# Hybrid encoder trunk, float32 in split halves: a wait ahead of the fourth weight tile's load, and two memory tiles rounded on VectorE

## The reference

```python
mem_n = rms_norm(mem, mem_norm)                     # 256 x 2048
for layer in range(DEPTH):                          # DEPTH = 2
    mem_k, mem_v = jnp.split(mem_n @ w_mem_kv[layer], 2, axis=-1)   # each 256 x 512
    ...  # layer 0: RMSNorm, input projection, conv + gated linear recurrence,
         #          memory attention, output projection, residual, shared K/V
    ...  # layer 1: the same frame with stick-breaking attention on the shared K/V
return rms_norm(h, final_norm)
```

## Time and profile before

| what | us |
|---|---|
| median of 3 runs | 1472.4 |
| lowest and highest of them | 1471.49, 1472.69 |
| the profiled execution | 1472.62 |
| its span, first to last instruction | 1470.5 |
| PE busy in the span | 1460.9 (99%) |
| DVE busy | 998.5 (68%) |
| ACT busy | 716.3 (49%) |

### The profile page before, as it was taken

The page is one execution under the profiler, slowest core; times in us unless marked ns, Lnnn a source line. Parts: engine busy times, 40 slices in busy tenths (PEclk is TensorE's granted clock), DMA queues, the critical chain, the costliest instruction groups (busy, mean ns, idle before and its releaser), DMA issues.

```text
span 1470.5 us, 18202 instructions
## 1 busy us (share of the span) xinstructions
PE 1460.9 (99%) x6840; PEld 1220.9 (83%) x6840; DVE 998.5 (68%) x1317; ACT 716.3 (49%) x1065; POOL 122.7 (8%) x184
## 2 busy tenths in 40 slices
PE   9999999999999999999999999999999999999997
PEld 7888888888888888888888888888888888888886
DVE  6775568465576896856578676566566556578987
ACT  6764544444544545763325654433333423455465
POOL 0001111111110000000010001111111111100000
PEclk9999999999999999999999999999999999999999
DMA  9877778776796887477999876777887977879853
GB/s 341 292 285 221 162 209 237 172 241 149 195 257 176 324 319 264 153 262 277 362 343 356 286 223 218 239 214 177 237 238 197 255 188 216 246 223 328 315 200 143
DMA packets 154190, 357.97 MB, mean 243 GB/s; under 512 B 7825, under 2 KB 23441, under 8 KB 150033
## 3 DMA queue, kind: packets, MB, share of 16 engines
q1 hardware_dynamic: 103824, 205.98, 40.3%
q0 software_dynamic: 29376, 102.77, 28.5%
q10 hardware_dynamic: 20928, 48.41, 9.0%
HBM read 310.99 MB, written 113.25 MB: 289 GB/s over the span
## 4 chain that ended last, share of the span: by engine, by line
PE 99%; DMA 1%; SPq 0%; ACT 0%; DVE 0%; issue 0%
PE main L2115 24%; PE main L2114 24%; PE main L2113 24%; PE aux L2114 5%; PE aux L2115 5%; PE aux L2113 5%; PE aux L2475 2%; PE aux L2421 2%; PE aux L2417 2%; PE aux L2419 2%; PE main L2421 1%; PE main L2417 1%; PE main L2419 1%; PE aux L2464 1%; DMA w_raw<-in_w_mem_kv 1%; PE aux L2257 0%
## 5 line engine op out<-in xcount | busy, mean ns | idle before, releaser
L2113 PE MATMUL main<-act_hi,w_hi 128*128 128x512 f32 x1216 | 475.5, 391 | 0.0
L2115 PE MATMUL main<-act_hi,w_lo 128*128 128x512 f32 x1216 | 473.9, 390 | 0.0
L2114 PE MATMUL main<-act_lo,w_hi 128*128 128x512 f32 x1216 | 473.6, 389 | 0.0
L2115 PEld LDWEIGHTS main<-act_hi,w_lo 128*128 128x128 f32 x1216 | 228.2, 188 | 47.9
L2114 PEld LDWEIGHTS main<-act_lo,w_hi 128*128 128x128 f32 x1216 | 228.4, 188 | 46.8
L2113 PEld LDWEIGHTS main<-act_hi,w_hi 128*128 128x128 f32 x1216 | 228.4, 188 | 46.6
L1320 DVE SCALAR_TENSOR_TENSOR w_lo<-w_raw,gains,w_hi 128x512 fp32r<-128x512 f32 x180 | 123.3, 747 | 120.9 <-ACT w_hi L698 120.9
L698 ACT ACTIVATE w_hi<-w_raw,gains 128x512 fp32r<-128x512 f32 x180 | 115.4, 712 | 141.1 <-PE main L2115 125.7
L1311 DVE TENSOR_TENSOR w_lo<-w_raw,w_hi 128x1024 fp32r<-128x1024 f32 x88 | 104.2, 1223 | 94.0 <-ACT w_hi L691 93.8
L691 ACT ACTIVATE w_hi<-w_raw 128x1024 fp32r<-128x1024 f32 x88 | 88.5, 1057 | 153.1 <-PE main L2115 109.5
L2113 PE MATMUL main<-w_hi,act_hi 128*128 128x512 f32 x336 | 131.1, 390 | 0.0
(11 more groups left out here) (325 smaller groups left out, 2081.3 us busy)
## 6 DMA issues: line engine op xcount, KB each, us to landing
w_raw<-in_w_in_a SPq DMA_DIRECT2D x32, 1024.0 KB, 8.3
w_raw<-in_w_in_b SPq DMA_DIRECT2D x32, 1024.0 KB, 7.3
weight_sums<-in_w_out_a POOLq DMA_DIRECT2D x48, 512.0 KB, 7.1
weight_sums<-in_w_out_b POOLq DMA_DIRECT2D x48, 512.0 KB, 7.8
weight_sums<-weight_sums POOLq DMA_DIRECT2D x32, 512.0 KB, 7.2
w_raw<-weight_sums SPq DMA_DIRECT2D x16, 1024.0 KB, 8.4
work<-weight_sums SPq DMA_DIRECT2D x16, 1024.0 KB, 7.5
w_raw<-in_w_mem_kv SPq DMA_DIRECT2D x13, 1024.0 KB, 5.1
```

The source lines that it names most:

```text
L2113: TE.matmul(o, a[0], b[0], start=first, stop=False)
L2114: TE.matmul(o, a[0], b[1], start=False, stop=False)
L2115: return TE.matmul(o, a[1], b[0], start=False, stop=final)
```

## The change

Two edits, both in the first 20 us of the program.

On SP, the wait for weight tile 0 moves from ahead of L494 to ahead of weight tile 3's load (L487). That load and all that stands behind it in SP's queue are now issued after weight tile 0 has landed.

Of slab 1's four memory tiles ACT rounds two (4 and 5) where it rounded four; DVE rounds tiles 6 and 7, as `V.tensor_copy` from float32 to fp32r. DVE's order in slab 1 becomes: low halves of memory tiles 4 and 5, of weight tile 4, then for k = 6 and 7: round memory tile k, its low half, and the low half of weight tile k - 1; then that of weight tile 7. A wait on ACT for all eight rounded memory tiles is added ahead of its slab 2 work, and one on DVE for the landing of slab 1's memory ahead of `low_tile(4)`.

```diff
--- before.py
+++ after.py
@@ -484,13 +484,13 @@
             sp.dma_start(w_raw[:, 0, 1, :], w_0[:, 1, :]).then_inc(w_first[1], 16)
             sp.dma_start(m_raw[0][:, 2 * M:], mem_t[0, :, NK + 2 * M:]).then_inc(m_loaded[0], 16)
             sp.dma_start(w_raw[:, 0, 2, :], w_0[:, 2, :]).then_inc(w_first[2], 16)
+            sp.wait_ge(w_first[0], 16)
             sp.dma_start(w_raw[:, 0, 3, :], w_0[:, 3, :]).then_inc(w_loaded[0], 16)
             load_mem(1)
             sp.dma_start(w_raw[:, 1, 0:2, :], w_1[:, 0:2, :]).then_inc(w_second, 16)
             sp.dma_start(w_raw[:, 1, 2:4, :], w_1[:, 2:4, :]).then_inc(w_loaded[1], 16)
             load_mem(2)
             sp.dma_start(four(1)[:, 0:2, :], w_2[:, 0:2, :]).then_inc(w_third, 16)
-            sp.wait_ge(w_first[0], 16)
             sp.dma_start(four(1)[:, 2:4, :], w_2[:, 2:4, :]).then_inc(w_first[0], 16)
             load_mem(3)
             for m in range(4):
@@ -786,13 +786,14 @@
                 nc.scalar.activation(w_hi[:, 0, k, :], w_raw[:, 0, k, :], ACT.Copy, scale=g_first[:, k:k + 1]
                                      ).then_inc(hi_ready, 1)
             act.wait_ge(m_loaded[1], 16)
-            for k in range(KS):
+            for k in range(2):
                 nc.scalar.activation(memt_hi[:, KS + k, :], m_tiles[1][:, k, :], ACT.Copy).then_inc(fill_hi, 1)
             for k in range(KS):
                 if k % 2 == 0:
                     act.wait_ge(w_loaded[1] if k else w_second, 16)
                 nc.scalar.activation(w_hi[:, 1, k, :], w_raw[:, 1, k, :], ACT.Copy, scale=g_first[:, KS + k:KS + k + 1]
                                      ).then_inc(hi_ready, 1)
+            act.wait_ge(fill_hi, 2 * KS)
             act.wait_ge(gains_loaded, 16)
             for m in range(4):
                 for j in range(4):
@@ -1445,10 +1446,15 @@
             for k in range(KS):
                 low_tile(k)
                 low_weights(k)
-            for k in range(KS, 2 * KS):
+            dve.wait_ge(m_loaded[1], 16)
+            low_tile(4)
+            low_tile(5)
+            low_weights(4)
+            for k in (6, 7):
+                V.tensor_copy(memt_hi[:, k, :], m_tiles[1][:, k - KS, :]).then_inc(fill_hi, 1)
                 low_tile(k)
-            for k in range(KS, 2 * KS):
-                low_weights(k)
+                low_weights(k - 1)
+            low_weights(7)
             dve.wait_ge(gains_loaded, 16)
             dve.wait_ge(const_step, 5)
             V.tensor_copy(ones_r[:], ones[:])
```

## The result

| | before | changed |
|---|---|---|
| median of 22 runs each, us | 1472.43 | 1474.20 |
| lowest and highest | 1471.49, 1473.84 | 1473.26, 1475.74 |
| the profiled execution | 1472.62 | 1473.62 |
| its span | 1470.5 | 1471.5 |

The ratio is 1.0012, with a 95% interval of 1.0006 to 1.0017: the changed kernel is 1.8 us slower (0.9 to 2.5). That is within the 0.2% that the prediction called no change and just inside its range (1471.5 to 1474.3), but three times its +0.6. The profiled execution, 1.0 us above that of before, is among the four fastest of the 22.

What follows compares the result with a forecast made beforehand. PE was taken to bound the kernel, with only its first slabs' starts open to change. Terms 0 (transfers), 0 (ACT), 0.5 (DVE at slab 2) and 0.1 (loads) gave +0.6 us: 1473.0 from 1472.4, range 1471.5 to 1474.3.

Steps and rivals of the forecast that it cites:

- What bounds the kernel: Whole kernel: PE holds 99% of the chain; only its starts in the first slabs matter, at most 1.15 us to gain.
- The engines don't run dry ... The term is 0: SP's moved wait: issues up to 0.9 us later are covered by bytes still queued; effect on the time 0.
- slab 1's weights land at 11.72 as before: Slab 1's weight load: bytes and order unchanged, engines moving 399 GB/s from 8.0 us on, so the landing stays at 11.72.
- the bounds given (-0.5 to +0.9): SP's moved wait: from 0.5 us sooner (tile 4 without its wait) to 0.9 us later (whole shift arrives).
- the cover fails: Rival at the first transfers: tile 3's bytes come late, 0.9 us arrives at tile 4; +1.5 to +1.8 in all, chance 0.19.
- a transfer behind can't hold back one ahead: DMA engines, first transfers: by ring order, the gain from fewer transfers in flight, up to 0.5 us at tile 4, would be nil.
- PE stalls 0.5 us: Slab 2's start: DVE's four added operations shift its first weight low half 1.10 us against 0.56 slack; bounds 0.4 and 0.8.
- I add 0.1 us for it (bounds 0 and 0.4): Later slab loads, slab 5 tightest: the loads' shift less PE's own takes 0.6 to 0.8 of its 0.62 us margin.
- the 0.2 that the prediction named as a sign of being wrong: Slabs 3 to 7: PE waits of more than 0.2 us would show the term for the loads wrong.
- the 1.1 to 1.3 reckoned with: Later slab loads on SP: expected to shift 1.1 to 1.3 us, as they wait for DVE's low halves.
- The margin: Slab 5: its first weight low half was ready at 33.88 for PE's 34.50, 0.62 us ahead.
- The sum: Whole kernel: 0 (transfers) + 0 (ACT) + 0.5 (DVE at slab 2) + 0.1 (loads behind) = +0.6 us.

Runs made afterwards that it cites:

- e8: Kernel before, with slab 1's memory loaded in two halves, each ahead of the weights that go with it; median 0.17 us below the kernel before (1.0000).
- e9: Kernel before, with slab 1's memory loaded in two halves and mem_nat's two loads two slab loads later; median 0.14 us below the kernel before (0.9998).
- e6: Second run of the kernel before with only SP's wait moved up, ahead of weight tile 3's load; median 1.25 us above the kernel before (1.0013).
- e1: Kernel before with only SP's wait moved up, ahead of weight tile 3's load; median 1.73 us above the kernel before (1.0010).
- e3: Changed kernel with both casts and low halves of memory tiles 6 and 7 ahead of weight tile 4's low half; median 2.09 us above before (1.0011).
- e5: Changed kernel with casts and low halves of tiles 6 and 7 ahead of weight tile 4's, SP's wait in its old place; +0.41 us on before (1.0004).
- e2: Changed kernel with SP's wait back in its old place, so only the two casts on DVE remain; median 1.01 us above the kernel before (1.0005).
- e10: Kernel before with SP's wait moved up, but behind weight tile 3's load; median 0.31 us above the kernel before (1.0003).
- e12: Changed kernel with mem_nat's two 1 MB loads issued two slab loads later on SP; median 2.00 us above the kernel before (1.0015).
- e4: Changed kernel with ACT rounding all four memory tiles again, DVE's new order and SP's moved wait kept; median 1.28 us above the kernel before (1.0009).
- e7: Kernel before with SP waiting for weight tiles 0 and 1 ahead of weight tile 3's load; median 1.90 us above the kernel before (1.0012).

## Why the prediction was right or wrong

The measured 1474.2 lies in the stated range with 0.1 us to spare, and that is luck: the forecast was +0.6 and the medians are +1.8 and +2.1. The term that was taken as 0, edit 1's, costs more than all that was counted.

**What bounds the kernel.** Right. In both profiles of the changed kernel nothing over 0.1 us is lost after 40 us, and emptying the waits ahead of tiles 1 to 3 gave nothing, since tile 4 hangs on the landing of slab 1's weights: 0.97 us were gained at tile 3 and none of them left at tile 4.

**Edit 1, "The engines don't run dry ... The term is 0".** This step failed. Its working was a mean rate and a byte count, and both held: withheld bytes did flow before the others ran out. What failed is the step from there to "slab 1's weights land at 11.72 as before": it took the rate of 399 GB/s as given whatever SP issues when. At 7 to 9 us, 3 to 5 us after SP resumed, the rate was 199 to 278 GB/s in all the seven profiles with edit 1's wait, and 389 to 409 in the five without one. And the loss isn't one number: where SP resumed 0.1 to 0.28 us later, slab 1's memory landed 0.7 to 1.9 us later. That is seven executions in two groups; that the later resume is the cause isn't shown. e8 and e9 speak for it: weight tile 0 landed as late as in e6, and without the wait nothing came late. The two profiles of the changed kernel, and e1's, fell among the early resumes, so a sum checked against the first profile alone would have called this term right. Of the bounds given (-0.5 to +0.9) tile 4 at 13.43 in e6 is 0.8 later than before, inside; 13.91 in e3 is not. The wait alone costs 1.25 and 1.73 us in the medians, and with the casts early 1.7 us (+2.09 in e3, +0.41 in e5).

The rival "the cover fails" (+1.5 to +1.8, at 0.19) named the median's size. Its mechanism was half right: the withheld transfers are late, though not for the latency of the first of them.

Weight tile 2 did land sooner: 4.3 to 4.7 us after its issue in the eight profiles in which weight tile 3 and all behind it were withheld, against 5.4 to 5.7 in before, e2, e5 and e10. So transfers behind do slow those ahead, here by about 1.1 us for one of 256 KB. (For tile 1 nothing is clear: 4.3 us in the changed kernel and 4.7 in before, but 3.7 in e10 and 3.8 in e5.) The Trainium skill (DMA: Bandwidth & Descriptors, section "Queues, rings and completion order") says that each DMA engine takes descriptors in ring order, and the prediction read from it that a transfer behind can't hold back one ahead. The landings disagree with that reading, and decide. The other rule, in the Trainium skill, same page, section "Rules for kernel authors", to issue early and wait late, was the better guide: these runs agree with it, by 1.25 and 1.73 us.

**Edit 2, "PE stalls 0.5 us".** Right, place, size and mechanism: slab 2 comes 0.5 us later after tile 4 with the casts behind the wait (6.04 against 5.55), and 0.2 us with them ahead (e5). DVE's starts were forecast at 16.74 and 17.88 and were 16.52 and 17.66, all of it because tile 4 itself came 0.1 sooner and DVE's small steps overlap. ACT's fill was forecast at 14.9 and began at 14.77, hidden as said.

**"I add 0.1 us for it (bounds 0 and 0.4)".** Place right, size wrong, mechanism half right: slab 5 lost 0.27 us at its start and 0.6 in all in the first profile, 0.9 and 1.1 in the second, beyond the 0.2 that the prediction named as a sign of being wrong. The load was issued 0.6 and 1.0 us later (25.33 and 25.67 against 24.71), less than the 1.1 to 1.3 reckoned with, but took 8.3 and 8.5 us to land where it had taken 7.6, which the sum left out. The margin was worked out from one landing. In e10 the same load, issued on time, took 8.8 us and slab 5 lost 0.5; in e2, with the casts, it took 8.1 and slab 5 lost next to nothing. So how much of slab 5's loss is the change's stays open.

**The sum.** 0.5 at slab 2 and 0.6 and 1.1 at slab 5, less the 0.1 and 0.2 by which tile 4 came sooner, make the 1.0 and 1.5 us of the two profiles. The median's 1.8 would need executions in which the transfers come late as well. The changed kernel's own two profiles show none; e12, which differs from it only in mem_nat's place, does, as do e3, e4 and e6. How the two edits add up stays open: apart they cost 1.25 to 1.73 and 1.01 us, together 1.77 and 2.14, and intervals of 1.3 us to either side can't say whether one hides part of the other. What makes the hole at 7 to 9 us stays open too. It goes with packets of 1 to 2 us, and with slow issuing: SP's longest issue in the same stretch took 0.9 to 1.2 us, against 0.43 at the start. Without the wait the longest took 0.7 to 1.0 us, at 4.6 to 6.6 us, where packets of 0.8 to 1.1 us are seen. Which of the two slows the other wasn't tried apart.

## What to carry to other kernels

A wait on a queue of transfers isn't covered just because bytes are still queued: read where the rate falls afterwards, and take more than one profile when the executions of a kernel spread wider than before, because the one you got may be the best of them. When work is given to an engine, put it into that engine's idle time, ahead of its wait, and not between two things that another engine waits for; the same four operations cost 0.5 us behind DVE's wait and 0.2 us before it. And a margin read from one landing is worth no more than that landing's spread.

## What was unexpected about the hardware

Withholding later transfers sped up those under way: 381 to 406 GB/s at 5 to 6 us with edit 1's wait, against 199 to 272 without. And single packets of 2 to 4 KB took up to 2.2 us while most took 0.08 to 0.16 us.

In two profiles a long wait of PE costs twice. After a listed wait of 2.20 us, up to 13.80 (e7), the granted clock was still full at 14 to 15 us and 0.50 at 16 to 18 us: 1.2 GHz, the lower of the two levels. Pairs of matmuls came 0.85 us apart instead of 0.46, and from tile 4 to slab 2 PE took 7.20 us instead of 5.55, another 1.6 us. After 2.60 us (e3) the clock was 0.50 at 16 to 19 us, and it took 7.47 us where the same order took 5.78 in e5, another 1.7 us. After 1.92 (e6), 1.8 (e4 and e12) and 1.25 us (the changed kernel) the granted clock stayed full.
